# Feed-forward of a six-layer transformer kernel: the zero matmuls that open the banks are dropped, and the last step is reordered on ScalarE and VectorE

## What is computed

```python
g, u = jnp.split(h @ w_gu, 2, axis=-1)      # 1024 -> 2 * 2816
return (jax.nn.silu(g) * u) @ w_down        # 2816 -> 1024
```

## Time and profile before

| | us |
|---|---|
| median of three runs | 1938.78 |
| lowest and highest run | 1938.53, 1939.84 |
| the profiled execution, its own time | 1939.04 |
| its span, first to last instruction | 1937.3 |
| PE busy (its share of the span) | 1885.9 (97%) |
| PEld busy | 1725.3 (89%) |
| DVE busy | 1344.6 (69%) |
| ACT busy | 973.7 (50%) |
| mean granted PE clock, as a share of full | 0.995 |
| DMA: moved, mean rate | 412.21 MB, 213 GB/s |

### The profile page before, as it was taken

How to read it: one execution, slowest core, us unless ns; L and a number is a source line. 1 busy time by engine, 2 the same in 40 slices (tenths; PEclk the granted TensorE clock), 3 DMA queues, 4 the chain that set the end, 5 groups by cost and what they waited for, 6 DMA issues and landing times.

```text
span 1937.3 us, 34589 instructions
## 1 busy us (share of the span) xinstructions
PE 1885.9 (97%) x13530; PEld 1725.3 (89%) x13530; DVE 1344.6 (69%) x2151; ACT 973.7 (50%) x1503; POOL 69.7 (4%) x82
## 2 busy tenths in 40 slices
PE   8999999999999999999999999999999999999998
PEld 7988999898899987899989799998989998979997
DVE  5757888774888876788878578886555555665555
ACT  6755333765533475633374453336654335665333
POOL 3003000000000000000000000002400000000000
PEclk9999999999999999999999999999999999999999
DMA  8528988532788842588853368875335554325552
GB/s 286 196 89 256 348 313 310 187 131 94 294 315 311 311 154 98 209 321 315 312 195 131 132 245 324 312 291 194 131 122 194 185 184 172 114 86 187 182 194 87
DMA packets 60354, 412.21 MB, mean 213 GB/s; under 512 B 8592, under 2 KB 8784, under 8 KB 11616
## 3 DMA queue, kind: packets, MB, share of 16 engines
q1 hardware_dynamic: 55728, 401.33, 56.3%
q0 software_dynamic: 4528, 9.56, 1.9%
HBM read 409.71 MB, written 3.16 MB: 213 GB/s over the span
## 4 chain that ended last, share of the span: by engine, by line
PE 82%; DVE 9%; ACT 4%; DVEq 2%; issue 2%; ACTq 1%; DMA 0%; SPq 0%
PE psu L502 34%; PE psy L665 17%; PE psy L564 6%; PE psy L556 5%; PE psy L610 5%; PE psu L519 3%; PE psm L740 3%; DVE wlo L859 2%; PE psu L725 2%; PE psy L543 2%; PE pso L711 1%; DVE ada_raw L1042 1%; DVE x L1109 1%; PE psy L633 1%; ACT whi L850 1%
## 5 line engine op out<-in xcount | busy, mean ns | idle before, releaser
L850 ACT CAST whi<-raw 128x2048 fp32r<-128x2048 f32 (+1 forms) x281 | 536.3, 1908 | 620.9 <-PE psu L502 421.7
L859 DVE TENSOR_TENSOR wlo<-raw,whi 128x2048 fp32r<-128x2048 f32 (+5 forms) x296 | 645.3, 2181 | 276.8 <-ACT whi L850 275.4
L502 PE MATMUL psu<-hhi,whi 128*128 128x256 f32 x1920 | 537.4, 280 | 0.0
L502 PE MATMUL psu<-hlo,whi 128*128 128x256 f32 x1920 | 536.4, 279 | 0.0
L502 PE MATMUL psu<-hhi,wlo 128*128 128x256 f32 x1920 | 536.3, 279 | 0.0
L502 PEld LDWEIGHTS psu<-hhi,whi 128*128 128x128 f32 x1920 | 361.2, 188 | 3.0
L502 PEld LDWEIGHTS psu<-hlo,whi 128*128 128x128 f32 x1920 | 361.2, 188 | 2.4
L502 PEld LDWEIGHTS psu<-hhi,wlo 128*128 128x128 f32 x1920 | 361.2, 188 | 0.0
L1042 DVE CUSTOM_DVE_ANT_0 ada_raw<-ada_raw,cvec 128x1024 f32<-128x1024 f32 x192 | 227.1, 1220 | 2.5 <-DMA ada_raw<-ada 2.5
L665 PE MATMUL psy<-whi,ahi 128*128 128x512 f32 x528 | 210.5, 399 | 1.0 <-DVE alo L1061 0.9
L665 PE MATMUL psy<-wlo,ahi 128*128 128x512 f32 x528 | 208.1, 394 | 0.0
(11 more groups left out here) (340 smaller groups left out, 3014.3 us busy)
## 6 DMA issues: line engine op xcount, KB each, us to landing
raw<-wts SPq DMA_DIRECT2D x280, 1024.0 KB, 4.8
ada_raw<-ada SPq DMA_DIRECT2D x96, 1024.0 KB, 4.8
dense_bias<-rel_bias POOLq DMA_DIRECT2D x32, 64.0 KB, 10.2
nab<-dense_bias SPq DMA_DIRECT2D x2, 1024.0 KB, 7.6
ada_raw<-fox_rows POOLq DMA_DIRECT2D x4, 512.0 KB, 9.1
cb<-cst POOLq DMA_DIRECT2D x1, 1408.0 KB, 8.6
cb<-cst SPq DMA_DIRECT2D x1, 1056.0 KB, 9.5
x<-x_in SPq DMA_DIRECT2D x2, 512.0 KB, 4.4
```

Of the source, the lines that this page charges most:

```text
L502: last = mm(psu[:, bank, cc * SEQ:(cc + 1) * SEQ], a[:, cols], h[:, kt, :], start=(kt == 0 and j == 0), stop=(kt == KT - 1 and j == 2))
L850: nc.scalar.copy(whi[:, part_of(c), 0:n], raw[:, slot_of(c), 0:n]).then_inc(hi_done, 1)
L859: last = nc.vector.tensor_tensor(wlo[:, part_of(c), cols], raw[:, slot_of(c), cols], whi[:, part_of(c), cols].bitcast(f32), ALU.subtract)
```

## The change

On PE the four opening matmuls go; the first turn of the loop is written out ahead of it, so that the first matmul of its first down unit into each `psy` bank has `start=True`; the loop runs from 1 to 5. On ACT, in the last step alone, silu of the last gu unit stands ahead of the high part of unit 33 (the first unit of the next stage) instead of behind it. On DVE the last step (gu 20 and 21, down 9, in the written-out turn) is written out: the first half step of ada comes first, behind a wait for the ada add before it; then the low part of unit 32, the activations of blocks 20 and 21, the second half step of ada, and the low part of unit 33.

```diff
@@ pe_ffn
-            def dn(c, i, s, aslot, last_step=False):
+            def dn(c, i, s, aslot, first_step=False, last_step=False):
...
-                                  start=False, stop=(last_step and ff == 1 and j == 2),
+                                  start=(first_step and ff == 0 and j == 0), stop=(last_step and ff == 1 and j == 2),
...
-            for b in range(4):
-                mm(fold(psy[:, b, :], 4, P), zeros[:], zeros[:].unsqueeze(1).to_broadcast([P, 4, P]),
-                   start=True, stop=False, skip_group_check=True)
-            with nc.tensor.Fori(0, 5) as i:
+            def turn(i, opens):
                 for k in range(2):
                     c = c0 + 2 + 3 * k
                     gu(c, i, 2 + 4 * i + 2 * k, par)
                     gu(c + 1, i, 3 + 4 * i + 2 * k, 1 - par)
-                    dn(c + 2, i, 2 * i + k, 2 * k).then_inc(unit_mm, 1)
+                    dn(c + 2, i, 2 * i + k, 2 * k, first_step=opens and k == 0).then_inc(unit_mm, 1)
+
+            turn(0, True)
+            with nc.tensor.Fori(1, 5) as i:
+                turn(i, False)
             dn(c0 + 32, 0, 10, 0, last_step=True).then_inc(unit_mm, 1)
@@ act_ffn
-            def silu(c, i, f, bank):
+            def silu(c, i, f, bank, last=False):
                 act.wait_ge(unit_mm, unit_no(l, c, i) + 1)
-                act_hi(act, l, c + SPLIT, i)
+                if not last:
+                    act_hi(act, l, c + SPLIT, i)
                 act.wait_ge(a_ready, n * NF + f - 1)
                 nc.scalar.activation(sg[:, bank], psu[:, bank, 0:SEQ], ACT.Silu).then_inc(silu_done, 1)
+                if last:
+                    act_hi(act, l, c + SPLIT, i)
...
-                    silu(c + 1, i, 3 + 4 * i + 2 * k, 1 - par)
+                    silu(c + 1, i, 3 + 4 * i + 2 * k, 1 - par, last=k == 1 and isinstance(i, int))
@@ dve_ffn
+            def last_step(i, k, c):
+
+                if a is not None:
+                    dve.wait_ge(ada_done, a * STEPS + 2 + 2 * i + k)
+                    dve_ada(dve, a, 2 + 2 * i + k, 0)
+                dve_lo(dve, l, c + SPLIT, i)
+                activations(2 + 4 * i + 2 * k, par, 2 - 2 * k)
+                activations(3 + 4 * i + 2 * k, 1 - par, 3 - 2 * k)
+                if a is not None:
+                    dve_ada(dve, a, 2 + 2 * i + k, 1)
+                dve_lo(dve, l, c + 1 + SPLIT, i)
+
             def turn(i):
                 for k in range(2):
                     c = c0 + 2 + 3 * k
+                    if k == 1 and isinstance(i, int):
+                        last_step(i, k, c)
+                        continue
                     for j in range(2):
                         dve_lo(dve, l, c + j + SPLIT, i)
                         activations(2 + j + 4 * i + 2 * k, par if j == 0 else 1 - par, 2 + j - 2 * k)
                         if a is not None:
                             dve_ada(dve, a, 2 + 2 * i + k, j)
-                    if k == 0 or not isinstance(i, int):
-                        dve_lo(dve, l, c + 2 + SPLIT, i)
+                    dve_lo(dve, l, c + 2 + SPLIT, i)
```

## The result

The changed kernel takes **1930.09 us** (median of six runs, 1928.29 to 1931.23), the kernel before 1938.65 (median of six, 1938.29 to 1943.36). The estimated ratio is 0.995, with a 95% interval of 0.9939 to 0.996, which leaves out 1: faster, by 0.44% between the medians. The profiled execution took 1930.56 us, with a span of 1928.8.

The account below looks back on a forecast made before the run. PE, busy 97% of the span, was taken as the bound. Opening 5.3, third and fourth ends 2.1, fifth 0.3, first two 0.9 make 8.6 us, from median 1938.78 to 1930.2; range 1928.8 to 1934.0.

Parts of the forecast that it names:

- Opening matmuls: PE, start of each feed-forward: four zero matmuls are wholly on the path, 0.88 us each time, 5.3 us in all six.
- First turn written out: PE's feed-forward loop: writing out its first turn costs and gives 0, since jumps back are free.
- (c): Rival, PE's loop: moved in code memory, each jump back fetches, 0.9 us each, 16 us; slower at 1946.4; chance 0.04.
- (e): Rival, PE's loop: the rule on jumps holds, each dropped jump gives 0.9 us, time 1924.8; chance 0.02.
- Last step, the stall: Feed-forward's end: last down's wait for the last activations goes, 0.46 us in four feed-forwards, 0.34 in the fifth.
- Last step, DVE's lag: End of third and fourth feed-forward: DVE no longer reaches the first psy bank late; 0.57 us goes in each.
- First and second: End of first two feed-forwards, paced by ACT's squares: last square comes earlier, 0.45 us each, 0.9 in all.
- What moves besides: High and low parts of unit 33, table load and SP's unit 36 load come later: cost 0, bound 2 us.

Follow-up runs that it names:

- e7: Kernel before with the four zero matmuls dropped, loop left as it was, no start flags, so the opening is left out; 1933.67 us, ratio 0.9964.
- e6: Kernel before with eight zero matmuls instead of four, nothing else changed; 1945.82 us, ratio 1.0026.
- e1: Kernel before with PE's part of the change alone (zero matmuls dropped, first turn written out), ACT and DVE as before; 1931.58 us, ratio 0.9958.
- e5: Kernel before with PE's first turn written out but the four zero matmuls kept and no start flag; 1939.29 us against 1940.24, ratio 1.0.
- e8: Changed kernel with all five turns written out on PE, no loop; 1929.88 us, ratio 0.9948 to the kernel before.
- e3: Kernel before with ACT's part alone: silu of the last block ahead of unit 33's high part, DVE in its old order; 1939.74 us, ratio 1.0001.
- e4: Kernel before with DVE's part alone: last step written out on DVE, ACT's order as before; 1938.9 us, ratio 0.9993.
- e10: Changed kernel with the whole low part of unit 33 made twice on DVE in the last step; 1937.11 us, ratio 0.9988 to the kernel before.
- e12: Changed kernel with 24 more long-met waits at the start of DVE's program, moving its later code; 1930.34 us, ratio 0.9952 to the kernel before.
- e2: Kernel before with ACT's and DVE's last-step parts alone, PE as before with its zero matmuls; 1932.8 us, ratio 0.9967.
- e9: Changed kernel with a quarter of the low part of unit 33 made twice on DVE in the last step; 1931.12 us.
- e11: Changed kernel with DVE's small column operation moved ahead of the gated update instead of behind it; 1929.26 us, ratio 0.9947 to the kernel before.

## Why the prediction was right, point by point

**Opening matmuls, 0.88 us in each of six.** Right. The changed kernel's distance is 0.23 instead of 1.11; e7 gives 0.88 to 0.97, e6 0.86 for four more. What was left open as bounds, 0.8 to 0.93, closes on 0.215 us a matmul. The slack behind it was read right as well: 2.0 us before, 1.1 now in the third feed-forward. In the first, ACT's wait for late loads was 25.4 us in seven places instead of 17.6 in five, without a wait on PE. That isn't shown to be the edit's doing: e1, with the same PE code, has 8.0, e5, with the four matmuls kept, 25.1, and all kernels lie between 3.7 and 25.4.

**First turn written out, 0.** Right: with 24 jumps back, with 18 (e5) and with none (e8, against the changed kernel's 18) the feed-forwards are of one length, and the packets of PE's code follow the code as written, so rivals (c) and (e) are out. The Trainium skill's rule ("Runtime: NRT & Kernel Launch", section on instruction fetch mechanics) has a stall for a jump whose target isn't in the fetched window; no run here shows such a stall on PE. One premise of the prediction was misread, without harm: PE's straight code in the mixers does have idles put down to "issue", three of 0.65 to 0.87 us at L610. They stand at the same three matmuls in every kernel of this case, e8 among them, whose PE code lies otherwise, so they are no fetches that hang on the place in PE's code.

**Last step, the stall.** The size (0.46, and 0.34 in the fifth) was right; the cause was told wrongly in part. The prediction said that "the reason stands on ACT", in the high part ahead of silu, and DVE's low part came second. e3 shows that ACT's order by itself is worth nothing, and e4 that DVE's order by itself ends the stall: the low part of unit 33 stood ahead of the activations. In the four feed-forwards with ada DVE was held even 0.1 us longer by its ada half than by ACT; in the fifth the low part did wait for the high part, as told. The row that says so stood in the prediction's own evidence: the low part starts at 970.47 with no idle ahead, while a wait for ACT of over 0.15 us would be shown in brackets. The sum came out because the change moves both.

**Last step, DVE's lag, 0.57 in the third and fourth.** Right in the third: DVE was to be free 0.5 us ahead of the first bank and is 0.60 ahead, and e10 turns the lag back on. In the fourth the sum was -1.91 and the measurement -1.63. The step that failed there is the silent assumption that both have the same tail: before, a pause of DVE's code (0.45 us) lay at the second L960, behind L633's start, and after at the first, ahead of it. e12, which moves it away, gets the 0.37 back and reaches -2.00; the 0.09 beyond -1.91 are the lead of the kernel before (below), and so is the fifth's -1.30 against -1.22.

**First and second, 0.45 each.** Measured 0.46 and 0.50 (their differences less 0.88), and 0.47 and 0.50 in e2. Right, and by the reason given: the second bank's square has no idle ahead of it any more, where it had 0.34, and the third waits for PE as before. ACT of the changed kernel:

```profile
341.55 0.58 ACT L875 ACTIVATE work<-psy 128x512 f32<-128x512 f32 x1
...
342.92 0.60 ACT L875 ACTIVATE work<-psy 128x512 f32<-128x512 f32 x1 [0.32 <-PE psy L665]
```

**What moves besides, 0.** Right for PE, ACT and SP. Not foreseen were two terms in the mixers that have nothing to do with the edits' purpose. They cancelled in the profiled execution, and so the total owes a part of its closeness to luck: either alone would have shifted it by about 1.5 us.

## What the runs showed of the hardware that was not expected

**Pauses in DVE's code.** DVE has idles of 0.40 to 0.47 us that nothing releases ("issue"), at single places. Two of them before, in the timeline of DVE at the end of the second mixer and in the sixth:

```profile
490.14 1.41 DVE L1002 SCALAR_TENSOR_TENSOR x<-rows,rs,x 128x512 f32<-128x512 f32 x2 [0.43 <-issue]
...
1729.45 0.29 DVE L802 TENSOR_TENSOR rows<-psm,rsum 128x128 f32<-128x128 f32 x1 [0.40 <-issue]
```

Both are gone in the changed kernel and in e2, which have the same DVE code, and both are there in e1, whose DVE code is the old one. More than that: the six kernels with the old DVE code (before, e1, e3, e5, e6, e7) have seven such idles, at the same seven instructions, and the four with the new (the changed kernel, e2, e4, e8) have two, at the same two. A pause can also hide in a wait. At the start of the second mixer DVE's first L919 stands 1.51 us behind the start of ACT's first piece, and 1.13 in the changed kernel, where PE's wait of 0.40 us behind it is gone:

```profile
350.29 1.93 ACT L909 ACTIVATE hhi<-psy,zcol,pcol 128x256 fp32r<-128x256 f32 x4 [1.43 <-PE psy L633]
351.80 0.48 DVE L919 SCALAR_TENSOR_TENSOR hlo<-psy,pcol,hhi 128x256 fp32r<-128x256 f32 x1 [1.98 <-ACT hhi L909]
```

```profile
350.17 1.94 ACT L910 ACTIVATE hhi<-psy,zcol,pcol 128x256 fp32r<-128x256 f32 x4 [1.42 <-PE psy L633]
351.30 0.48 DVE L920 SCALAR_TENSOR_TENSOR hlo<-psy,pcol,hhi 128x256 fp32r<-128x256 f32 x1 [1.60 <-ACT hhi L910]
```

For PE's starts these places are worth -0.38 and -0.35 in the second mixer, -0.48 in the fifth (the pause at the second L960) and -0.30 in the sixth: in all -1.5 us. (The second mixer is only 0.50 shorter, since its half-clock stretch gives back 0.27.) In e2, e4 and e8, the other kernels with new DVE code, the second mixer gains the same at both places, and the fifth and sixth are shorter by 0.43 to 0.48 and 0.32 to 0.35; in e1, e3, e5, e6 and e7 nothing of it shows. e12 shows that 24 instructions of nothing are enough to move such a pause. What happens in the pause, the runs don't show; that it is a fetch of code is argued from the place alone. PE shows none in the feed-forwards (e8).

**Starts further apart in the lead.** In some feed-forwards PE's starts stand about 1% further apart all through the lead, at a granted clock of 1.00: 118.7 ns on average instead of 117.6 in the first, 123.2 instead of 122.3 from the third on. That costs 0.09 us, and 0.20 where it goes on through the two gu units behind the lead (117.8 instead of 116.7). The kernel before has it in the fourth and fifth lead, the changed kernel nowhere, e1 in the first and fourth (0.20 each), e2 in the third, e6 in the fourth, e9 in the fifth (0.20) and e10 in the fourth and fifth (0.20 each). This is where the table's odd tenths come from, such as the -0.09 of e5. No run shows its cause.

**The clock of PE in three attention stretches.** Between the first 13 us and the last 6 of the span the granted clock is 1.00 almost everywhere. It falls to half (1.2 instead of 2.4 GHz) for 3.4, 6.8 or 10.2 us in the first three mixers, in the kernel before behind waits of PE for ACT of 3.25, 3.25 and 1.89 us (L784 twice, L1695). The stretches of before, and then those of the changed kernel: span, busy us (and count) of PE, PEld, DVE, ACT, POOL, granted clock, DMA share, GB/s.

```profile
103.50:106.90 3.40, 3.40 (x19) 3.40 (x18) 1.34 (x7) 1.47 (x5) 0.00 (x0) 0.50 0.25 106
438.00:444.80 6.80, 6.19 (x28) 5.37 (x29) 2.90 (x9) 2.50 (x10) 0.00 (x0) 0.50 0.35 145
728.10:731.50 3.40, 3.40 (x18) 3.40 (x18) 0.90 (x5) 1.36 (x6) 0.00 (x0) 0.50 0.09 36
```

```profile
101.10:107.90 6.80, 5.74 (x26) 4.91 (x27) 3.36 (x11) 2.95 (x10) 0.00 (x0) 0.50 0.43 158
439.00:445.80 6.80, 6.80 (x34) 6.62 (x32) 2.33 (x10) 2.65 (x7) 0.00 (x0) 0.50 0.24 101
725.80:729.20 3.40, 3.40 (x18) 3.40 (x18) 1.20 (x7) 1.17 (x5) 0.00 (x0) 0.51 0.16 65
```

The changed kernel had 3.4 us more of it in the first mixer, which is 1.22 us longer; 1.06 of them lie at that stretch, and 0.20 in the kernel's first 14 us, a part that differs by -1.1 to +0.5 between the kernels though their code there does the same. e1 and e2 had no half-clock stretch in the third mixer, where e1's row reads

```profile
725.50:728.80 3.30, 3.30 (x31) 3.30 (x31) 1.92 (x12) 2.20 (x8) 0.00 (x0) 1.00 0.10 40
```

(31 matmuls in 3.3 us, against 18 at half clock), and that mixer is 1.55 us shorter in both, behind the same wait of PE (1.88 us in e1). e3 had none there either, with the same 1.55, nor had e7, e10, e11 and e12; the changed kernel and e4, e5, e6, e8 and e9 had it. So it goes with no edit. Over the kernels, 3.4 us more or less of half clock were worth 1.0 to 1.6 us. It explains why the medians of e1 and e2 don't add up, and probably, though no run shows it, the spread of 3 us within a kernel's runs. In e10, where PE waited 2.17 us for the late norm, one more stretch appeared at 982.3 us, and the mixer behind it was 0.5 us longer; in e6 one more lay in the sixth mixer, which is 1.54 us longer.

## What to carry to other kernels

Read a queue's order from the idle in brackets before blaming the engine upstream: an instruction that starts without idle was held by its own engine, and moving its producer gains nothing (e3), as moving the engine's own order alone only shifts the wait (e4). Work that others don't need goes behind the last thing they do need, on every engine of the chain at once. For changes of a few microseconds, cut the trace at fixed instructions and compare stretches: the total carried 1.5 us of code placement and 1.3 us of clock that the stretches tell apart.
